# One core, a two-block transformer: three fox tiles per weight chunk in the opening loop, and the steps around it in another order

## The reference, cut to what matters

```python
mod = silu(c) @ w_ada + b_ada                   # 1024 x 6144: shift, scale, gate, twice
h = rms(x) * g * (1 + sc1) + sh1
u = h @ w_in                                    # fq, fk, fv (512 each), fg (8), dq, dk, dv (512 each)
fq, fk = rms(heads(fq)), rms(heads(fk))         # per head of 64
log_f = log_sigmoid(fg + b_f)                   # forget gate, cumulated along the tokens
fox   = softmax(fq fk^T / 8 + cum_i - cum_j) fv # 8 heads, causal
dq, dk = rms(dq), rms(dk)
diff  = (softmax(q1 k1^T + alibi) - lam * softmax(q2 k2^T + alibi)) dv   # 4 heads
x = x + g1 * (concat(fox, rms(diff) * (1 - lam_init)) @ w_out)
x = x + g2 * ((silu(h2 @ w_gate) * (h2 @ w_up)) @ w_down)
```

## Time and profile before

| what | value |
|---|---|
| median of 3 runs | 811.13 us (810.12 to 812.34) |
| the profiled execution: its time | 810.03 us |
| the profiled execution: its span, first to last instruction | 808.3 us |
| mean granted TensorE clock | 0.995 |
| PE busy | 772.3 us, 96% of the span |
| DVE busy, ACT busy | 461.9 us (57%), 388.6 us (48%) |
| moved by DMA | 158.73 MB, 196 GB/s on the mean |

### The profile page before, as it was taken

The page is one execution under the profiler, slowest core; times in us unless marked ns, Lnnn a source line. Parts: engine busy times, 40 slices in busy tenths (PEclk is TensorE's granted clock), DMA queues, the critical chain, the costliest instruction groups (busy, mean ns, idle before and its releaser), DMA issues.

```text
span 808.3 us, 10238 instructions
## 1 busy us (share of the span) xinstructions
PE 772.3 (96%) x3969; PEld 615.6 (76%) x3969; DVE 461.9 (57%) x592; ACT 388.6 (48%) x543; POOL 60.5 (7%) x75
## 2 busy tenths in 40 slices
PE   4898999999999999999999999999999999999995
PEld 2566776658888889888878887777888888888884
DVE  3366676557565546365594545655756656445364
ACT  3254756535444335345544357655545454434252
POOL 2004020010000000001270000000010000000001
PEclk9999999999999999999999999999999999999998
DMA  9998346997556256665769454333555555554601
GB/s 281 299 362 280 105 152 247 366 359 253 168 201 200 90 180 235 208 211 181 259 199 321 145 171 153 106 127 133 157 179 185 171 182 183 184 184 154 208 27 52
DMA packets 86786, 158.73 MB, mean 196 GB/s; under 512 B 5227, under 2 KB 23876, under 8 KB 84691
## 3 DMA queue, kind: packets, MB, share of 16 engines
q1 hardware_dynamic: 84402, 151.09, 55.8%
q0 software_dynamic: 2128, 6.90, 2.6%
q10 hardware_dynamic: 208, 0.08, 0.0%
HBM read 156.99 MB, written 1.08 MB: 196 GB/s over the span
## 4 chain that ended last, share of the span: by engine, by line
PE 81%; issue 6%; DVE 3%; SPq 3%; ACT 3%; DMA 3%; POOL 1%; POOLq 0%; DVEq 0%; ACTq 0%
PE PS L874 25%; PE PS L876 24%; PE PS L875 24%; PE PS L1002 3%; DMA raw<-in_w_ada 2%; ACT whi L1173 1%; DVE wlo L1385 1%; SPq L804 1%; PE PS L1072 1%; PE PS L1043 1%; SPq L792 1%; PE PS L1098 1%; DMA g_dram<-mod 1%; PE PS L962 1%; SPq L777 1%
## 5 line engine op out<-in xcount | busy, mean ns | idle before, releaser
L1385 DVE TENSOR_TENSOR wlo<-raw,whi 128x2048 fp32r<-128x2048 f32 (+1 forms) x126 | 280.2, 2226 | 188.0 <-ACT whi L1173 160.4
L1173 ACT ACTIVATE whi<-raw 128x2048 fp32r<-128x2048 f32 (+1 forms) x126 | 227.1, 1804 | 151.5 <-PE PS L876 151.5
L874 PE MATMUL PS<-whi,hT 128*128 128x512 f32 (+1 forms) x704 | 279.4, 397 | 2.4 <-issue 1.9
L876 PE MATMUL PS<-whi,hT 128*128 128x512 f32 (+1 forms) x704 | 272.2, 387 | 0.0
L875 PE MATMUL PS<-wlo,hT 128*128 128x512 f32 (+1 forms) x704 | 272.0, 386 | 0.0
L874 PEld LDWEIGHTS PS<-whi,hT 128*128 128x128 f32 x704 | 133.1, 189 | 33.3 <-issue 8.6
L876 PEld LDWEIGHTS PS<-whi,hT 128*128 128x128 f32 x704 | 132.8, 189 | 27.2
L875 PEld LDWEIGHTS PS<-wlo,hT 128*128 128x128 f32 x704 | 133.1, 189 | 23.9
L874 PE MATMUL PS<-whi,hidT 128*128 128x512 f32 x216 | 84.5, 391 | 0.0
L876 PE MATMUL PS<-whi,hidT 128*128 128x512 f32 x216 | 84.1, 389 | 0.0
L875 PE MATMUL PS<-wlo,hidT 128*128 128x512 f32 x216 | 84.1, 389 | 0.0
(11 more groups left out here) (224 smaller groups left out, 639.3 us busy)
## 6 DMA issues: line engine op xcount, KB each, us to landing
raw<-in_w_in SPq DMA_DIRECT2D x36, 1024.0 KB, 5.1
raw<-in_w_ff SPq DMA_DIRECT2D x32, 1024.0 KB, 5.2
raw<-in_w_ada SPq DMA_DIRECT2D x16, 1024.0 KB, 6.6
raw<-in_w_gate SPq DMA_DIRECT2D x10, 1024.0 KB, 5.6
raw<-in_w_up SPq DMA_DIRECT2D x10, 1024.0 KB, 5.2
raw<-in_w_down SPq DMA_DIRECT2D x10, 1024.0 KB, 5.0
raw<-in_w_ada SPq DMA_DIRECT2D x16, 512.0 KB, 7.1
raw<-in_w_out SPq DMA_DIRECT2D x8, 1024.0 KB, 5.0
```

The source lines that it names most:

```text
L874: pe.matmul(o, ah, wh, start=(k == 0), stop=False)
L876: return pe.matmul(o, al, wh, start=False, stop=end)
L1173: act.activation(split_view(whi, i), slab_view(raw, slot, i), ACT.Copy).then_inc(hi_made, 1)
L1385: dve.tensor_tensor(split_view(wlo, i), slab_view(raw, slot, i), whole(split_view(whi, i)), ALU.subtract).then_inc(lo_made, 1)
```

## The change

- In the loop a slab of `w_in` has 1536 columns, and each chunk has three pieces, one for each fox tile (24 pieces in place of 16). Slabs 8 and 9 of before are gone: from here on slab numbers are two lower, and slab 8 is the first of diff 0. `whi` and `wlo` hold one such slab per slot. Fox 2 accumulates in banks 4 and 5; the `rows` products go to the chunk's own bank, 6 or 7, where the transposes follow.
- A turn of the loop is now: `rows` of chunk j+1, the fox 0 piece of chunk j, `xT` and `col` of chunk j+1, its `split` and then its `part0`, the fox 1 and fox 2 pieces of chunk j. Before it was: fox 0 piece of chunk j, `rows` of chunk j+2, fox 1 piece of chunk j, `xT`, `col`, `part0` and `split` of chunk j+2.
- `setup`, `relbias` and `vectors` stand inside the loop, after chunks 3, 4 and 5; `relbias` and `vectors` use banks 6 and 7 in place of 4 and 5.
- Behind the loop: one split behind `evac` of fox 0, then `fgate`, `unit` 0, `unit` 1, `logf`, and the next split.
- The whole of diff 0 stands ahead of `scores` 0. `ada` 8 to 14 stand between pieces of diff 1 and diff 2, 15 to 18 between pieces of `w_out`. `BETWEEN` has fewer fillers for most units. `unit` 3 stands right behind `evac` of diff 1.
- The load of `alibi` moves from `relbias` to behind `unit` 1 on POOL.

```diff
-BETWEEN = {"fox": (2, 1, 1, 2, 2), 1: (2, 1, 1, 2, 1), 2: (2, 1, 1, 1, 1), 3: (2, 0, 1, 1, 1),
-           "diff": (2, 0, 1, 0, 1), 7: (1, 0, 1, 0, 1),
+BETWEEN = {"fox": (2, 1, 0, 1, 1), 2: (2, 0, 1, 1, 1), 3: (2, 0, 1, 1, 0), "diff": (2, 0, 1, 0, 1), 6: (2, 0, 1, 0, 0), 7: (1, 0, 1, 0, 0),
...
-    order += [("cond", 0), ("chunk", 0), ("sums0", 0), ("norm", 0), ("rows", 0), ("early", 0), *early, ("xT", 0), *column(0)]
-    order += [*rows(1), ("xT", 1), *early, *column(1)]
+    order += [("cond", 0), ("chunk", 0), ("sums0", 0), ("norm", 0), ("rows", 0), ("early", 0), ("xT", 0), ("col", 0), *early,
+              ("part0", 0)]
     for j in range(KC):
-        slabs.append(dict(weight="w_in", row=j * P, chunks=1, col=0, cols=2 * W))
-        pair = [("piece", dict(T=fox[n], k=j, slab=j, off=n * W, first=n == 0, last=n == 1)) for n in range(2)]
-        if j < KC - 2:
-            order += [pair[0], *rows(j + 2), pair[1], ("xT", j + 2), *column(j + 2), *early]
-            order += {KC - 4: [("setup", 0)], KC - 3: early + [("relbias", 0)]}.get(j, [])
-        elif j == KC - 2:
-            order += [pair[0], *early, ("vectors", 0)]
-            second = pair[1]
+        slabs.append(dict(weight="w_in", row=j * P, chunks=1, col=0, cols=3 * W))
+        step = [("piece", dict(T=fox[n], k=j, slab=j, off=n * W, first=n == 0, last=n == 2)) for n in range(3)]
+        if j < KC - 1:
+            order += rows(j + 1) + step[:1] + [("xT", j + 1), ("col", j + 1), *early, ("part0", j + 1)]
+            order += step[1:]
+            order += {KC - 5: [("setup", 0)], KC - 4: [("relbias", 0)], KC - 3: [("vectors", 0)]}.get(j, [])
         else:
-            order += [pair[0], ("evac", fox[0]), second, pair[1], ("evac", fox[1])]
-    order += early + [("fgate", 0), ("unit", 0), ("logf", 0), ("unit", 1)]
-    now = whole("fox", 2, "w_in", 2 * W, "h")
-    order += insert(now, (4, early), (6, [("heads", 0)]))
+            order += step[:1] + [("evac", fox[0])] + early + step[1:2] + [("evac", fox[1])]
+            order += step[2:] + [("evac", fox[2])]
+    order += [("fgate", 0), ("unit", 0), ("unit", 1), ("logf", 0)] + early
     tail = []
     for n in range(3):
         tail += whole("diff", n, "w_in", 3 * W + FOX + n * W, "h")
-    tail = insert(tail, (11, [("unit", 2)]), (20, [("unit", 3)]), (23, ada[8:10]))
+    tail = insert(tail, (4, early), (6, [("heads", 0)]), (7, early), (9, [("scores", 0), ("heads", 1), ("lam", 0)]),
+                  (12, [("unit", 2)]), (18, [("unit", 3)]), *[(13 + 2 * j, [ada[8 + j]]) for j in range(7)])
     wo = [tile("w_out", n, KC, "mix") for n in range(2)]
     fill = slab(wo[0], "w_out", 0, 0) + slab(wo[1], "w_out", W, 0)
-    tail += insert(fill, *[(j, [ada[10 + j]] + ([("grow", 0)] if j == 5 else [])) for j in range(8)])
-    order += [("scores", 0), ("heads", 1), ("lam", 0)] + tail[:3]
-    tail = tail[3:]
-    order += attention(list(range(FOX_P + DIFF_P)), tail, ada[18:20])
+    tail += insert(fill, *[(2 * j, [ada[15 + j]] + ([("grow", 0)] if j == 2 else [])) for j in range(4)])
+    ahead = tail.index(("lam", 0)) + 4
+    order += tail[:ahead]
+    tail = tail[ahead:]
+    order += attention(list(range(FOX_P + DIFF_P)), tail, ada[19:20])
...
                 elif kind == "relbias":
...
-                    take(4)
-                    pe.matmul(PS[0:MOBA, 4, 0:SKEW], table[:, :], hot[:, :], start=True, stop=True).then_inc(rel_ps, 1)
-                    reader[4] = [(rel_row, 1)]
+                    take(6)
+                    pe.matmul(PS[0:MOBA, 6, 0:SKEW], table[:, :], hot[:, :], start=True, stop=True).then_inc(rel_ps, 1)
+                    reader[6] = [(rel_row, 1)]
```

More of the change, by code:

```diff
@@ L172, in plan @@
     ada = [("ada", j) for j in range(3 * KC)]
-    fox = [tile("fox", n, KC, "h") for n in range(2)]
-    def column(j):
-        return [("col", j), ("part0", j)]
+    fox = [tile("fox", n, KC, "h") for n in range(3)]
     def rows(j):
@@ L617, in home @@
         def home(s):
-            return (s // 2 % SPL, s % 2) if s < KC else ((s - KC // 2) % SPL, 0)
+            return s % SPL
         def split_view(t, s):
-            slot, half = home(s)
-            return t[:, slot, half * 2 * W:half * 2 * W + SLABS[s]["chunks"] * SLABS[s]["cols"]]
+            return t[:, home(s), 0:SLABS[s]["chunks"] * SLABS[s]["cols"]]
         def slabs_under(s):
-            slot, half = home(s)
-            under = [e for e in range(s) if home(e)[0] == slot and (e >= KC or s >= KC or home(e)[1] == half)]
-            return under[-1] + 1 if under else 0
+            return max(0, s - SPL + 1)
         def landed(eng, it):
@@ L863, in _ @@
                         pe.wait_ge(lo_made, s + 1)
-                    if k == 0 and T >= 2:
-                        for ready in tile_readers(T - 2):
+                    if k == 0 and tile_under(T) >= 0:
+                        for ready in tile_readers(tile_under(T)):
                             pe.wait_ge(*ready)
+                    if (T, k) == (2, 0):
+                        take(4, 5)
                     operand_ready(T, k)
@@ L893, in _ @@
                         last.then_inc(gemm_done, 1)
-                    elif (T, k) == (0, KC - 1):
+                    elif T < 2 and k == KC - 1:
                         last.then_inc(first_done, 1)
+                    if (T, k) == (2, KC - 1):
+                        reader[4] = reader[5] = tile_readers(T)
                 elif kind == "cond":
@@ L919, in _ @@
                     last.then_inc(rows_ps, 1)
-                    reader[b] = [(row_in, i + 1)]
                 elif kind == "xT":
                     b = chunk_bank(i)
-                    take(b)
+                    pe.wait_ge(row_in, i + 1)
                     pe.wait_ge(xn_act, 1)
@@ L936, in _ @@
                     for a in range(2):
-                        last = pe.matmul(PS[:, chunk_bank(i), S + a:S + a + 1], row_of(i)[:, a * P:(a + 1) * P], sel[:, :],
+                        last = pe.matmul(PS[:, chunk_bank(i), a:a + 1], row_of(i)[:, a * P:(a + 1) * P], sel[:, :],
                                          start=True, stop=True)
                     last.then_inc(col_ps, 1)
+                    reader[chunk_bank(i)] = [(aff_made, i + 1)]
                 elif kind == "vectors":
                     pe.wait_ge(vec_in, 16 * NROWS)
-                    take(5)
-                    pe.transpose(PS[:, 5, 0:V_ALL], vec[:, :], ident[0:V_ALL, 0:V_ALL]).then_inc(vec_ps, 1)
-                    reader[5] = [(col_made, 1)]
+                    take(7)
+                    pe.transpose(PS[:, 7, 0:V_ALL], vec[:, :], ident[0:V_ALL, 0:V_ALL]).then_inc(vec_ps, 1)
+                    reader[7] = [(col_made, 1)]
                 elif kind == "relbias":
@@ L1182, in _ @@
                         act.wait_ge(col_ps, i - 1)
-                    act.activation(row_of(i), PS[:, 4 + i % 2, 0:256], ACT.Copy).then_inc(row_in, 1)
+                    act.activation(row_of(i), PS[:, chunk_bank(i), 0:256], ACT.Copy).then_inc(row_in, 1)
                 elif kind == "part0":
@@ L1432, in _ @@
                     dve.wait_ge(vec_ps, 1)
-                    then(dve.tensor_copy(col[:, V_LN2:V_ALL], PS[:, 5, V_LN2:V_ALL]))
+                    then(dve.tensor_copy(col[:, V_LN2:V_ALL], PS[:, 7, V_LN2:V_ALL]))
                     dve.tensor_scalar(col[:, V_ALL:V_ALL + 1], col[:, V_QK:V_QK + 1], HD ** -0.5, None, ALU.mult)
@@ L1864, in _ @@
                     inverse_root(hrs[:, i, :], hss[:, i, :], HD).then_inc(hrs_made, 1)
+                    if i == 1:
+                        pool.wait_ge(part_lo, KC)
+                        pool.dma_start(alibi[:, :, :], A["constants"][:, C_ALIBI:C_HOT].rearrange("p (h k) -> p h k", h=DIFF)
+                                       ).then_inc(alibi_in, 16)
                 elif kind == "grow":
```

24 lines of the change are left out of this document (11 added, 13 removed).

## The result

| | kernel before | changed kernel |
|---|---|---|
| median, first measurement | 810.62 us (808.37 to 812.34, 4 runs) | 822.93 us (818.78 to 823.22, 4 runs) |
| median, measured again later (experiment 5) | 809.86 us (807.68 to 811.44, 21 runs) | 820.42 us (818.34 to 821.30, 5 runs) |
| profiled execution: time, span, clock | 810.03, 808.3, 0.995 | 818.78, 817.0, 0.989 |

The ratio is 1.0146 [1.0125 to 1.0166] in the first measurement and 1.0130 [1.0112 to 1.0149] in the second: slower, by 1.3 to 1.5%. The prediction was 818.4 (810.5 to 822.5). The second median lies in the range, the first 0.4 us above it. The two profiled executions lie 8.75 us apart (predicted 7.3).

The account below looks back on a forecast made before the run. The kernel was taken as bound by PE with holes. Slab 9's 0.5 plus the attention's 6.8 gave 7.3 us on the profiled 810.03, or 817.3; the median stands 1.1 higher, so 818.4 us, range 810.5 to 822.5.

Parts of the forecast that it names:

- The loop: Loop over chunks: PE sets late turns at 5.95 us, `relbias` and `vectors` add 2.7 us; chunk 7 comes at 56.9.
- T: The time at which the last fox 0 piece behind the loop ends, forecast at 64.6 us.
- Rival (c): Loop bound by transfers, 5.7 to 6.5 us a turn, ending 3 us later: 821.5 us; chance 0.14 together with (d).
- Slab 9: Behind the loop: its split is ready at T+18.0, PE stands 6.1 us, half clock costs 1.6; 0.5 us late at `scores` 0.
- keys first: Behind the loop, `unit` 1 (the keys' scaling) stands ahead of `logf`; said to cost 1.5 us of slab 9's chain.
- The port: SBUF port behind the loop: `unit` 0 runs beside POOL's root (second row); exclusion (first row) would add 1.2 us, chance 0.05.
- The attention: From `scores` 0 to `w_out`'s second half: new PE waits sum to 13.95 against 4.1 before; 6.8 us late, ends 0 and 9.8.
- fall into the new waits: In the attention, some 3 us of PE's small gaps between operations before are absorbed, taking 9.8 us late to 6.8.
- with it 1.4 for a clock that falls again: In the attention, PE's lower clock behind the 3.65 us wait at `scores` 3 costs 1.4 us.
- (a): Rival: the attention keeps its 4.1 us of waits, only 0.5 us is lost, 811.6 us; chance 0.12.
- (b): Rival: packs between diff pieces remove the attention's waits, 807.5 us; a lower slab 9 wait would help likewise; chance 0.12.
- (d): Rival: fox 2's pieces lengthen the loop by their own 10.9 us, losing its 3 us gain: 821.5; chance 0.14 with (c).

Follow-up runs that it names:

- experiment 5: The changed kernel run again with nothing edited: 820.42 us, ratio 1.0130 to the kernel before.
- Experiment 2: Changed kernel with slab 9's split put ahead of `fgate`: 813.67 us, ratio 1.0052 to the kernel before.
- experiment 1: Changed kernel with `logf` put back ahead of `unit` 1: 818.38 us, ratio 1.0111 to the kernel before.
- experiment 7: Changed kernel with 14 products that nothing reads put on PE ahead of its wait at `scores` 3: 817.08 us, ratio 1.0086 to the kernel before.
- experiment 3: Changed kernel with `unit` 3 two pieces later, behind `scores` 3: 816.69 us, ratio 1.0091 to the kernel before.
- experiment 4: Changed kernel with both slab 9's split ahead of `fgate` and `unit` 3 two pieces later: 809.44 us, ratio 0.9999 to the kernel before.
- experiment 9: Changed kernel with `relbias` and `vectors` moved from the loop to behind it, ahead of `fgate`: 826.04 us, ratio 1.0196 to the kernel before.

## Why the prediction was right, point by point

**The loop.** Chunk 5 was said to come at 42.3 and came at 42.27; chunk 7 at 56.9 and came at 56.70; T at 64.6, measured 64.4. The turns from chunk 2 to 5 are 6.0 to 6.16 us apart (5.95 said). `relbias` and `vectors` cost 1.47 + 0.76 us above a normal turn of 6.1, together 2.2 where 2.7 stood. "PE sets the late turns" held, but "no wait for DMA" is the exception: chunk 3 waited in eight of ten executions (experiment 5). The marks agree this well because they come from one of the other two. Rival (c) was right about the kind of wait, but its 3 us are too large: in seven of the eight the loop ended 0.2 to 0.9 us later.

**Slab 9.** Ready at T+18.0 said, T+17.9 measured; PE stood for 5.66 us where 6.1 was said. Experiment 2 shows the mechanism by its removal. The wait was not caused by keys first (1.4 us of it, experiment 1), but by putting the split behind the whole chain when the eight pieces that had covered it were gone. `scores` 0 were predicted for 90.2 and came at 90.04.

**The port.** The choice of the second row over the first was right for this place: `unit` 0 began at 72.73 and took 1.21 us beside POOL's root. By the rule of the Trainium skill, "SBUF — State Buffer", section "SBUF: two separate sides", it would have started at 75.2.

**The attention.** It was said to end 6.8 us late. From `scores` 0 to the second half of `w_out` it takes 85.86 us (175.90 - 90.04) where before took 77.8 (89.74 to 167.53), so it is 8.1 us late. The long waits were found at their places: `scores` 1 1.25 us (2.0 said), the first `probsT` 1.90 (2.4), `scores` 3 3.56 (3.65), the third pair's `probsT` 1.27 (1.7). Seven small ones take 1.75 together, where four small ones stood at 2.8. Their sum is 9.73. The walk gave 12.55, and less the 3 us of small gaps that "fall into the new waits" that is 9.55. So the sum of the waits is right, but partly by luck, since the reason for the 3 us is not shown: the 4.1 us that PE stood idle before are six waits (1.57, 0.36, 0.51, 0.22, 0.63 and 0.79), which leaves nothing for small gaps. What they made good is that the walk had the waits too long, by 2.8 us in all. **The step that failed is the term "with it 1.4 for a clock that falls again"**: experiment 7 shows 3.1 us. With the measured terms the step's sum is 9.73 + 3.1 - 4.1 = 8.7, against the 8.1 measured; the 0.6 between them is open.

**The sum.** 7.3 us were said for a profiled execution, and 8.75 are measured; the clock behind `scores` 3 alone is 1.7 us more than its term. But this execution is the best case. By the ratios the changed kernel is 10.5 to 11.8 us slower, so that the size was off by 3 to 4.5 us. For the median 818.4 was said, and two measurements gave 822.9 and 820.4. The changed kernel's executions scatter more than those of before, and the fastest was the profiled one. Two of the causes are shown by experiment 5, and neither had a term: the wait of chunk 3 for its transfer, and the clock that falls behind `probsT` in most executions (1.2 us). A third is the clock behind slab 9, at 1.8 to 2.5 us instead of 1.6. What lifts some executions to 823 is open.

**The rivals.** (a) fell: PE is idle for 9.5 us between 90 and 175 us. The waits were of order, and experiments 2 and 3 moved them by order alone, at an unchanged load. (b) fell at the point that it named: `unit` 3 and POOL's root alone cost 3.56 us and the clock behind them. But experiment 4 shows that its remark on slab 9 was half right. With both waits out the kernel is back at the time of before, not at 807.5. (d) fell: T came when the forecast said.

## What to carry to other kernels

When work that covered a chain is moved ahead of it, count what now stands between the chain's start and the first step that needs its end; here eight pieces had covered two splits and a logarithm. To a wait of TensorE like the two long ones here (5.7 and 3.6 us) add what the pieces behind it lose at half clock: 1.8 to 3.1 us here, once nearly as much as the wait itself. And follow a moved step on every engine's list, also on those whose time is cheap: a copy of 0.54 us put ahead of `fgate` cost 4.19 us on PE and held POOL's first root back by 7.4 us.

## What the runs showed of the hardware

- The low clock cost more behind the shorter wait. Behind 5.66 us of idling PE had its full clock again some 3.5 us after its first product, behind 3.56 us only after 6.9 us. The low clock as such was equally long in both places, 6.8 us (worked out from the windows below; those between them are at 0.50). At slab 9 it fell 2.4 us after PE had stopped, so that 3.3 us of it passed while PE stood. At `scores` 3 it fell only as PE began again, and all of it fell on work:

```profile
78.00:80.00 2.00, 0.00 (x0) 0.00 (x0) 0.57 (x2) 2.00 (x2) 0.00 (x0) 0.74 0.22 88
...
84.00:86.00 2.00, 2.00 (x6) 1.52 (x5) 0.35 (x1) 0.00 (x0) 0.00 (x0) 0.55 1.01 376
...
122.00:124.00 2.00, 0.78 (x8) 0.78 (x10) 2.00 (x4) 0.00 (x0) 0.00 (x0) 0.84 0.00 0
...
130.00:132.00 2.00, 2.00 (x18) 1.26 (x16) 0.00 (x0) 0.93 (x3) 0.00 (x0) 0.96 0.96 397
```

- With the same waits ahead of it (1.25 us at `scores` 1 and 1.9 us at `probsT`), PE's clock fell in the execution of experiment 5 (and in five others) and stayed in the one shown first. The same program can so come out over 1 us apart. The Trainium skill, "TensorE: Matmul & The Clock Gate", section "Part 1: The HAM clock gate (the "warmup" mystery)", says that the number of slow products at the start of one and the same kernel differs from run to run. The two traces show such a difference in the middle of a kernel, behind waits.
- Products that nothing reads, put into a wait, kept the clock at 1.00 in both places and brought more than they cost. Against the second measurement of the changed kernel the ratios give 3.2 and 3.6 us, with intervals that just overlap; the traces show a gain of 1.3 us up to `scores` 0 for the first (the loop's shift taken off) and 3.1 us for the second.
- POOL's short scaling (0.20 us at other times) took 1.35 us at 76.09 in experiment 9, where DVE's `unit` 0 ran from 76.16 to 77.37, as it took 1.91 us beside DVE's split in the earlier trace rows. DVE's operation was not slowed in either case, nor beside POOL's root. What the rule of the Trainium skill quoted above says held here for POOL's short operation and not for DVE's, and not in its order either: in experiment 9 POOL's began 0.07 us ahead of DVE's and was yet the one that took long.
